# The place of TensorE's moving rows within 256 bytes: 128 bytes past the weights' place in place of 192

## The reference

```
first_block:   hn = rmsnorm(x); proj = hn @ w_in + b_in          # 2048 x 11272
               mLSTM heads, a gated convolution, two branch products, gates
               h = x + merged @ w_out
               u = causal_dwconv(rmsnorm(h) @ w_up, ...)          # 2048 x 11008
               h = h + (silu(gate) * val) @ w_down                # 5504 x 2048
second_block:  h = concat([meta_tokens, h]);  proj = rmsnorm(h) @ w_in_2   # 2048 x 10240
               pooling mixer, RG-LRU (two gate products per head), gelu, gates
               h = h + merged @ w_out_2
               h = h + square(relu(rmsnorm(h) @ mlp_w1)) @ mlp_w2 # 2048 x 8192 x 2048
out = rmsnorm(h)[:, 16:]
```

## Time and profile before

| | |
|---|---|
| median of 3 runs | 2846.65 us (2838.86, 2846.65, 2859.54) |
| the profiled execution | 2872.7 us |
| its span, first to last instruction | 2870.9 us |
| TensorE busy | 2759.9 us, 96% |
| VectorE busy | 1712.2 us, 60% |
| ScalarE busy | 1297.9 us, 45% |
| instructions | 53233, of them 22994 matmuls |
| DMA | 503.22 MB, mean 175 GB/s |

### The profile page before, as it was taken

How to read it: one execution, slowest core, us unless ns; L and a number is a source line. 1 busy time by engine, 2 the same in 40 slices (tenths; PEclk the granted TensorE clock), 3 DMA queues, 4 the chain that set the end, 5 groups by cost and what they waited for, 6 DMA issues and landing times.

```text
span 2870.9 us, 53233 instructions
## 1 busy us (share of the span) xinstructions
PE 2759.9 (96%) x22994; PEld 2740.0 (95%) x22994; DVE 1712.2 (60%) x1729; ACT 1297.9 (45%) x1448; POOL 1.8 (0%) x14
## 2 busy tenths in 40 slices
PE   4999999999999999999999977999999999999998
PEld 4899999999999999999889977999999999999998
DVE  4455464566667466646785757756665555455555
ACT  3444454444544344435553466444454334343343
POOL 0000000000000000000000000000000000000000
PEclk8999999999999999999999988999999999999999
DMA  4345555555555555555445433565555565655653
GB/s 154 129 150 176 180 187 190 181 186 180 188 191 187 181 189 177 191 189 172 155 169 180 151 115 118 183 198 191 196 188 188 189 182 187 191 183 185 186 182 116
DMA packets 257817, 503.22 MB, mean 175 GB/s; under 512 B 10150, under 2 KB 19038, under 8 KB 257630
## 3 DMA queue, kind: packets, MB, share of 16 engines
q1 hardware_dynamic: 254592, 500.20, 53.2%
q10 hardware_dynamic: 3054, 0.55, 0.1%
HBM read 498.63 MB, written 2.10 MB: 174 GB/s over the span
## 4 chain that ended last, share of the span: by engine, by line
PE 88%; DVE 7%; ACT 3%; ACTq 1%; issue 1%; DVEq 0%
PE psum L470 27%; PE psum L471 27%; PE psum L472 27%; PE psum L497 2%; PE psum L498 2%; PE psum L499 2%; DVE wlo L1095 2%; DVE work L1123 1%; ACTq L753 1%; ACT whi L767 1%; DVE work L1485 1%; ACT misc L1005 0%; DVE hn L1133 0%; DVE misc L1531 0%; ACT hn L788 0%
## 5 line engine op out<-in xcount | busy, mean ns | idle before, releaser
L1095 DVE TENSOR_TENSOR wlo<-raw,whi 128x1024 fp32r<-128x1024 f32 x952 | 1160.4, 1223 | 1010.2 <-ACT whi L767 1008.6
L767 ACT ACTIVATE whi<-raw 128x1024 fp32r<-128x1024 f32 x952 | 1003.4, 1058 | 1351.0 <-PE psum L472 1233.5
L470 PE MATMUL psum<-hn,whi 128*128 128x256 f32 x4448 | 1255.3, 282 | 33.0 <-DVE wlo L1095 24.9
L471 PE MATMUL psum<-hn,whi 128*128 128x256 f32 x4448 | 1252.0, 281 | 0.0
L472 PE MATMUL psum<-hn,wlo 128*128 128x256 f32 x4448 | 1251.7, 281 | 0.0
L470 PEld LDWEIGHTS psum<-hn,whi 128*128 128x128 f32 x4448 | 850.6, 191 | 38.1 <-DVE wlo L1095 26.7
L472 PEld LDWEIGHTS psum<-hn,wlo 128*128 128x128 f32 x4448 | 848.4, 191 | 0.0
L471 PEld LDWEIGHTS psum<-hn,whi 128*128 128x128 f32 x4448 | 842.5, 189 | 0.1
L470 PE MATMUL psum<-act,whi 128*128 128x256 f32 x2544 | 716.3, 282 | 12.4 <-DVE wlo L1095 7.5
L471 PE MATMUL psum<-act,whi 128*128 128x256 f32 x2544 | 715.3, 281 | 0.0
L472 PE MATMUL psum<-act,wlo 128*128 128x256 f32 x2544 | 715.3, 281 | 0.0
(11 more groups left out here) (210 smaller groups left out, 976.7 us busy)
## 6 DMA issues: line engine op xcount, KB each, us to landing
raw<-in_w_in SPq DMA_DIRECT2D x160, 1024.0 KB, 5.1
raw<-in_mlp_w SPq DMA_DIRECT2D x128, 1024.0 KB, 5.4
raw<-in_w_up SPq DMA_DIRECT2D x80, 1024.0 KB, 5.0
raw<-in_w_down SPq DMA_DIRECT2D x40, 1024.0 KB, 5.1
raw<-in_w_out SPq DMA_DIRECT2D x32, 1024.0 KB, 5.1
raw<-in_w_branch_m SPq DMA_DIRECT2D x8, 1024.0 KB, 5.0
raw<-in_w_branch_c SPq DMA_DIRECT2D x8, 1024.0 KB, 5.0
raw<-in_w_up SPq DMA_DIRECT2D x8, 768.0 KB, 4.4
```

What stands on the lines that cost most here:

```text
L470: mm(o, hi[:, kk, w], both[:, 0, :], start=first and m % 2 == 0, stop=False)
L471: mm(o, hi[:, kk, w], both[:, 1, :], start=False, stop=False)
L767: A(whi[:, n % SLOTS, :], raw[:, n // 2 % RAW, n % 2 * HALF:(n % 2 + 1) * HALF], ACT.Copy)\
L1095: V.tensor_tensor(wlo[:, n % SLOTS, :], raw[:, n // 2 % RAW, n % 2 * HALF:(n % 2 + 1) * HALF], whi[:, n % SLOTS, :].bitcast(F32), ALU.subt ...
```

## The change

The unused array between `h` and `hn` gets 32 elements in each partition where it had 48, that is 128 bytes in place of 192. All arrays behind it move by 64 bytes. `raw`, `whi`, `wlo` and `h` stay.

```diff
         h = sb("h", [P, NT, T])
 
-        sb("gap_a", [P, 48])
+        sb("gap_a", [P, 32])
         hn = sb("hn", [P, NT, MAIN + 2 * T], F32R)
```

## The result

| | before | after |
|---|---|---|
| median | 2845.97 us (2838.86 to 2859.54, 4 runs) | 2918.74 us (2914.10 to 2919.45, 4 runs) |
| profiled execution | 2872.7 us | 2914.1 us |

The kernel is slower: ratio 1.0246, 95% interval 1.0207 to 1.0286. That is 73 us more by the medians. The runs after also spread less, 5 us where those before spread 21.

A forecast was written before the change was run, and what follows sets the result against it. The prediction took TensorE's spacing between matmuls to bound the kernel. With 117.76 ns for every 256-column matmul, 2872.7 + 4.0 x 4.43 gave 2890 us; the range was 2792 to 2919 us.

The forecast's parts named there:

- the rest of the change: Wide and gate matmuls, other engines, waits and DMA: 0 us, but for 4 us either way on the wide matmuls.
- the wide stream: The 1536 matmuls of 272 columns at L497 to L499, read before the change as 125.7 ns each.
- The sum: Time from narrow (256-column) matmuls at spacing p: 2872.7 + 17.0 x (p - 117.76) + 4.0 x (p - 113.33) us.
- p: Spacing in ns of the 256-column matmuls with moving rows at 128 bytes; taken as 117.76.
- the long rhythm: The slower spacing of 256-column matmuls before the change, 117.76 ns, forecast for all of them; chance 0.32.
- the two terms: 17.0 thousand matmuls counted from 117.76 ns and 4.0 thousand from 113.33 ns, each times the change in spacing.
- the prediction's own sign: Test of the mechanism: wrong if spacing is neither 113.3, 117.8 nor 119 ns, or if idle time appears before L470.
- (C): Rival: 256-column matmuls pay the 272-column surplus of 12.3 ns, 119.1 ns each, 2919 us; chance 0.10.
- The picture behind the choice of sign: Moving rows and next weights meet twice per matmul, about 5 ns each, except at 192, where one meeting can fall between matmuls.
- The rule of two independent ports: TensorE reads moving operand and weights independently, so no place within 256 bytes matters and time stays at the median.
- The estimate of 2710 us: From the page's N/2.4 + 2.5 ns, 109.2 ns for 256 columns: 2872.7 - 146 - 16, a stream without meetings.
- Rival (B): No change: TensorE's rhythms come from interruptions, not the place; 2846 us, 2820 to 2873; chance 0.25.

The follow-up runs named there:

- rest_back: Kernel after the change with 64 unused bytes behind act, so only hn and act stay moved; 2905.53 us, ratio 1.0155 to before.
- weights_moved: Kernel after the change with 64 unused bytes ahead of whi, so hn, act and all behind are at their old addresses; 2918.44 us, ratio 1.0188 to before.
- place0: Kernel before the change without the gap, moving rows beginning at the weights' own place within 256 bytes; 2929.87 us, ratio 1.0312 to before.
- few_columns: Matmul-only kernel with 64, 128 and 192 columns in place of 256, plus 256 at distance 112; 111.4 to 111.8 ns for few columns at full clock.

## Why the prediction came out as it did

- That TensorE's spacing is what one matmul costs, that the same instructions run in two rhythms, and that the rest of the change is worth nothing: right. The idle times, the other engines' durations (1223 and 1058 ns for a half chunk, as before) and the wide stream (125.9 ns) are unchanged, and rest_back and weights_moved leave only the distance.
- The sum is right but for some 7 us. The mean spacing of all narrow matmuls at full clock after is 119.23 ns over the trace, for which it gives 2872.7 + 25.0 + 23.6 = 2921 us; the profiled execution took 2914.1, and place0 was 7 us under its sum too. The granted clock can account for that after the change: the share of the clock not granted, times the span, is 50 us before and 41 after.
- The step that failed is the value of p. I took the nearest row of the same shape, the long rhythm at 117.76 ns, and forecast 2890 us. It measured 118.65 and 120.0, so the two terms together were +18 us where they should have been +49. By the prediction's own sign a spacing that is neither 113.3 nor 117.8 nor 119 says that the mechanism is wrong, and 120.0 is such a spacing; the 834 and 843 matmuls in 100 us are what it named for (C). Rival (C), the surplus of the wide matmuls (119.1 ns, 2919 us), had the size, at a chance of 0.10. It deserved more: the wide stream was the only row that had rows at 128. Its closeness is partly chance, as 272 columns have a table of their own, 123.3 to 126.7, and as the 125.7 ns behind it count the two matmuls cut by the edges (the earlier trace rows give 126.1 without them, and (C) would be some 8 us more). That the median of 2918.74 us is within the stated range, by 0.3 us, rests on (C) alone and is luck.
- The picture behind the choice of sign (two meetings at every place but 192, one at its edge) gave the right sign for 128 and is wrong as it stands, so the sign too was in part luck. 64 has 192's two rhythms, 112 has the short one alone, 32 has 116.7, and 512 columns pay 13 to 21 ns. Nor is the 6.7 ns over 106.7 one meeting: some 5 of it are there with 64 columns as well, at the 111.7 of few_columns. What is shown is that the spacing hangs on the distance of the two operands within 256 bytes, on the sequence of rows, and on how the stream was entered. That TensorE's two read streams get in each other's way is the natural reading of it; no trace shows the reads themselves. The law behind the table stays open.
- The rule of two independent ports, which the prediction took from the Trainium skill, "TensorE: Matmul & The Clock Gate", Part 2, step 1, doesn't describe this case: the traces differ by up to 6.7 ns a matmul (120.0 against 113.3) from the place alone. The estimate of 2710 us from the 109.2 ns of "Back-to-back issue gap" on that page (a formula that the page gives for a single matmul apart) wasn't reached either: no block with a weight load for each matmul is under 111.4 ns.
- Rival (B), in which the rhythm was a matter of interruptions alone: half of it is true. At 192, 64 and 128 the interruption decides between two, and the blocks at 16, 80, 144, 160 and 208 differ from one interruption to the next as well; which spacings there are, the place decides.

## What to carry to other kernels

Where float32-format matmuls with a weight load each follow one another without a gap, count the matmuls in 100 us instead of reading the mean duration, and look whether stretches of the same code differ. If they do, or if the spacing is above columns / 2.4 GHz, measure all sixteen distances of 16 bytes between moving rows and weights in a small kernel without any computation, several interruptions each, and take one with a single fast rhythm; a gap in units of 64 bytes would have missed it here. A kernel whose runs spread over 1% at a steady clock may owe that to such rhythms, and then a median of three runs can't judge a change of 1%: here 32 bytes, with 116.7 ns throughout, came out 1% slower than before, though it is faster than the long rhythm of 192.

## What the runs showed of the hardware

- The spacing of 256-column float32-format matmuls at full clock depends on the distance of their two operands within 256 bytes: from 113.3 ns (112) to about 120 (0, 96, at times 80 and 128) at multiples of 16 bytes, and to 123.3 at others. At half clock it is 213.3 ns at 192 and at 0 (place0), with no surplus in either.
- The same stream at the same addresses can run in one of two rhythms (113.3 and 117.8 ns at 192 and 64, 118.7 and 120.0 at 128), and kept the one it fell into for as long as 700 us.
- A matmul with a weight load of 128 columns in this format took 111.4 to 111.8 ns at full clock with 64, 128 and 192 columns, whatever the place, and 213.3 ns at the lower clock with 64 and 128.
- The traffic of VectorE, ScalarE and the DMAs (175 GB/s) doesn't set these spacings: the blocks with nothing beside them have those of the whole kernel, to some 0.3 ns at 0, 32, 64, 112, 128 and 192.
